# A two-block network on one core: the first modulation product as one phase of whole tiles instead of two halves

## What is computed

```python
c_act = jax.nn.silu(c)
mod = c_act @ w_ada[l] + b_ada[l]
sh1, sc1, gt1, sh2, sc2, gt2 = jnp.split(mod, 6, axis=-1)
u = _modulate(h, g_mix[l], sh1, sc1)
h = h + gt1[:, None, :] * _hybrid_mixer(u, w_in[l], ...)
u = _modulate(h, g_ffn[l], sh2, sc2)
h = h + gt2[:, None, :] * _conv_ffn(u, w_up[l], ...)
```

## Time and profile before

| what | value |
|---|---|
| median of 3 runs | 2468.82 us |
| the profiled execution | 2468.61 us, span 2466.8 us |
| PE busy, share of the span | 99% |
| PE weight loads | 81% |
| DVE, ACT, POOL busy | 47%, 37%, 43% |
| HBM read, whole kernel | 244.76 MB, 100 GB/s over the span |

### The profile page before, as it was taken

How to read it: one execution, slowest core, us unless ns; L and a number is a source line. 1 busy time by engine, 2 the same in 40 slices (tenths; PEclk the granted TensorE clock), 3 DMA queues, 4 the chain that set the end, 5 groups by cost and what they waited for, 6 DMA issues and landing times.

```text
span 2466.8 us, 32936 instructions
## 1 busy us (share of the span) xinstructions
PE 2453.8 (99%) x11477; PEld 2005.9 (81%) x11477; DVE 1168.4 (47%) x1728; ACT 914.3 (37%) x1307; POOL 1070.8 (43%) x529
## 2 busy tenths in 40 slices
PE   9999999999999999999999999999999999999999
PEld 6877888888888888877888888888888777888887
DVE  7574867256331345676330345331345666431332
ACT  4444443235322334555321334321234554431332
POOL 5332454444444445334444445444445334443444
PEclk9999999999999999999999999999999999999999
DMA  6223653332233331322232332233231332232332
GB/s 254 87 75 98 225 180 114 114 97 85 85 103 104 100 101 61 103 77 94 83 108 99 100 101 71 85 106 107 94 110 61 92 88 94 77 103 92 94 107 81
DMA packets 74062, 253.47 MB, mean 103 GB/s; under 512 B 9184, under 2 KB 13408, under 8 KB 73856
## 3 DMA queue, kind: packets, MB, share of 16 engines
q1 hardware_dynamic: 73408, 251.93, 31.6%
q10 hardware_dynamic: 576, 0.52, 0.1%
HBM read 244.76 MB, written 2.10 MB: 100 GB/s over the span
## 4 chain that ended last, share of the span: by engine, by line
PE 84%; issue 9%; DVE 3%; POOL 3%; ACT 1%; DMA 0%; SPq 0%; POOLq 0%; DVEq 0%; ACTq 0%
PE unit_bank L671 25%; PE unit_bank L673 25%; PE unit_bank L672 25%; POOL w_lo L530 2%; PE score L779 2%; PE score L769 1%; DVE arena L1772 1%; PE mix L672 1%; PE mix L673 1%; PE mix L671 1%; PE mix L927 1%; PE out_bank L906 1%; PE out_bank L726 0%; DVE arena L2521 0%; PE mix L1005 0%
## 5 line engine op out<-in xcount | busy, mean ns | idle before, releaser
L530 POOL TENSOR_TENSOR w_lo<-raw,w_hi 128x1024 fp32r<-128x1024 f32 (+2 forms) x374 | 953.8, 2550 | 1295.5 <-ACT w_hi L1268 1295.4
L1268 ACT ACTIVATE w_hi<-raw 128x1024 fp32r<-128x1024 f32 (+2 forms) x375 | 416.5, 1111 | 1163.9 <-PE unit_bank L673 1122.0
L671 PE MATMUL unit_bank<-u_hi,w_hi 128*128 128x512 f32 x2142 | 840.9, 393 | 0.4 <-POOL w_lo L530 0.4
L673 PE MATMUL unit_bank<-u_hi,w_lo 128*128 128x512 f32 x2142 | 835.2, 390 | 0.0
L672 PE MATMUL unit_bank<-u_lo,w_hi 128*128 128x512 f32 x2142 | 835.1, 390 | 0.0
L671 PEld LDWEIGHTS unit_bank<-u_hi,w_hi 128*128 128x128 f32 x2142 | 402.4, 188 | 93.6 <-issue 9.5
L673 PEld LDWEIGHTS unit_bank<-u_hi,w_lo 128*128 128x128 f32 x2142 | 402.4, 188 | 84.0
L672 PEld LDWEIGHTS unit_bank<-u_lo,w_hi 128*128 128x128 f32 x2142 | 402.6, 188 | 81.8 <-issue 0.2
L671 PE MATMUL unit_bank<-h_hi,w_hi 128*128 128x512 f32 x915 | 357.6, 391 | 0.2 <-DVE h_lo L2200 0.2
L673 PE MATMUL unit_bank<-h_hi,w_lo 128*128 128x512 f32 x915 | 356.6, 390 | 0.0
L672 PE MATMUL unit_bank<-h_lo,w_hi 128*128 128x512 f32 x915 | 356.6, 390 | 0.0
(11 more groups left out here) (422 smaller groups left out, 2176.7 us busy)
## 6 DMA issues: line engine op xcount, KB each, us to landing
raw<-in_w_gate_up SPq DMA_DIRECT2D x168, 512.0 KB, 3.5
raw<-in_w_down SPq DMA_DIRECT2D x64, 704.0 KB, 4.1
raw<-in_w_in SPq DMA_DIRECT2D x65, 512.0 KB, 3.5
raw<-in_w_up SPq DMA_DIRECT2D x30, 512.0 KB, 3.5
f<-in_w_ada_rows SPq DMA_DIRECT2D x26, 512.0 KB, 4.8
raw<-in_w_out SPq DMA_DIRECT2D x24, 512.0 KB, 3.6
raw<-in_w_down SPq DMA_DIRECT2D x16, 512.0 KB, 3.5
ada_in_u<-in_w_ada SPq DMA_DIRECT2D x8, 512.0 KB, 11.2
```

The lines of the kernel that those rows point to most:

```text
L530: e.tensor_tensor(w_lo[:, s, 0:n], raw[:, s, 0:n], as32(w_hi[:, s, 0:n]), ALU.subtract).then_inc(lo_ready, 1)
L671: e.matmul(bank[:], wh, hi(k), start=begin and n == 0, stop=False)
L673: mm = e.matmul(bank[:], wl, hi(k), start=False, stop=end and last)
L1268: e.activation(w_hi[:, s, 0:n], raw[:, s, 0:n], ACT.Copy).then_inc(hi_ready, 1)
```

## The change

w_ada is loaded in eight transfers of 1 MB, whole rows of 2048 columns in pieces of 8 KB, all of them issued ahead of the three tiles of w_in. Four land in the place of u_hi and u_lo, three in h, one in slots 16 to 19. `ada_part(k)` multiplies 512 columns into each quarter of the bank, once per k. The row has 512 columns, four transposes turn it, and DVE needs two short operations (`take_turned`, `amplify`) instead of two times three. `modulate` runs over all 8 chunks in one go. One part of `grow` stands ahead of it and one behind. POOL does all four doublings ahead of its splits. The group products are ordered anew: for each chunk the highs and rests of two units, the low of the first, and from the third chunk on the third unit two chunks behind; then the rest of the low parts.

```diff
-            load_ada_first(0, ada_loaded)
+            for k in range(DC):
+                e.dma_start(ada_first[k], d["w_ada"][k]).then_inc(ada_loaded[k], 16)
             for s in range(2):
                 load(0, s, d["w_in"][s], D)
             e.dma_start(third_raw[:], d["w_in"][2]).then_inc(third_loaded, 16)
-            load_ada_first(1, second_loaded)
...
-            for n in (1, 2):
+            for n in (1, 2, 4, 8):
                 double(n)
                 square_angle()
+            e.sem_inc(turn_ready, 1)
             split_pair(IN1, D)
             e.wait_ge(hi_ready, 3)
             e.tensor_tensor(third_lo[:], third_raw[:], as32(third_hi[:]), ALU.subtract).then_inc(lo_ready, 1)
-            e.wait_ge(B_padded, 1)
-            for n in (4, 8):
-                double(n)
-                square_angle()
-            e.sem_inc(turn_ready, 1)
...
-            def ada_part(half, k):
+            def ada_part(k):
...
                 for q in range(4):
-                    mm = e.matmul(out_bank[32 * q:32 * q + 32, 0:2 * P], c_act[:, k:k + 1].broadcast_to([P, 32]),
-                                  ada_first[half][k][:, 2 * P * q:2 * P * (q + 1)], start=k == 0, stop=k == DC - 1)
+                    mm = e.matmul(out_bank[32 * q:32 * q + 32, :], c_act[:, k:k + 1].broadcast_to([P, 32]),
+                                  ada_first[k][:, T * q:T * (q + 1)], start=k == 0, stop=k == DC - 1)
...
-                elif k == 5:
+                elif k == 4:
                     e.wait_ge(x0_inverse, 1)
...
-                else:
-                    keep_warm(2)
-            turn_ada(0, score[0], 2)
-            keep_warm(12, out_bank)
+                elif k < DC - 1:
+                    keep_warm(4)
+            turn_ada(0, score[0], TB)
+            keep_warm(10, out_bank)
...
+            e.wait_ge(uhi_ready, 1)
             for s in range(2):
                 e.wait_ge(hi_ready, s + 1)
                 e.wait_ge(taken[s], 1)
+                group_high(s, 0)
+            for c in range(1, DC):
+                both(group_high, c, uhi_ready)
+                both(group_rest, c - 1, u_ready)
+                e.wait_ge(lo_ready, 1)
+                group_low(0, c - 1)
+                if c >= 2:
+                    e.wait_ge(hi_ready, 3)
+                    group_high(2, c - 2)
+                    group_rest(2, c - 2)
+            both(group_rest, DC - 1, u_ready)
+            group_low(0, DC - 1, True)
+            e.wait_ge(lo_ready, 2)
+            for c in EIGHT:
+                group_low(1, c, c == DC - 1)
+            for c in (DC - 2, DC - 1):
                 group_high(2, c)
                 group_rest(2, c)
+            e.wait_ge(lo_ready, 3)
+            for c in EIGHT:
                 group_low(2, c, c == DC - 1)
...
-            take_row(DC, 0, out_bank[:, 0:2 * P])
+            take_row(DC, 0, out_bank[:])
             for s in range(2):
                 refill(IN1, s)
-            for s in range(2):
-                shifted(0, s)
+                shifted(s)
             e.wait_ge(third_loaded, 16)
             e.activation(third_hi[:], third_raw[:], ACT.Copy).then_inc(hi_ready, 1)
-            for c in range(2, 4):
-                shifted(0, c)
-            take_row(2 * DC, 1, out_bank[:, 0:2 * P])
-            for c in range(4, DC):
-                shifted(1, c)
+            for c in range(2, DC):
+                shifted(c)
...
-            take_half(0)
-            e.wait_ge(x0_spread, 1)
-            modulate(range(4))
             power_of_lam(2, 2)
             e.wait_ge(zeroed, 1)
-            grow(B_grown, STRIDE, b_bar[:, 0, :, :], b_bar[:, 1, :, :], False)
+            grow(B_grown, STRIDE, b_bar[:, 0, :, :], b_bar[:, 1, :, :], False, (0,))
+            take_turned(1, 0, score[0])
+            amplify(0, "g_mix", 8)
+            e.sem_inc(mod_ready, 1)
+            e.wait_ge(x0_spread, 1)
+            modulate(range(DC))
+            grow(B_grown, STRIDE, b_bar[:, 0, :, :], b_bar[:, 1, :, :], False, (1,))
             e.sem_inc(B_padded, 1)
-            take_half(1)
-            modulate(range(4, DC))
```

More of the change, by code:

```diff
@@ L208, in program @@
         ada_in_f = f.rearrange("p (n c) t -> p n (c t)", c=4)
-        ada_first = [[ada_in_u[:, k, :] for k in range(DC)],
-                     [ada_in_h[:, k, :] for k in range(6)] + [slot(16, 2), slot(18, 2)]]
+        ada_first = [ada_in_u[:, k, :] for k in range(4)] + [ada_in_h[:, k, :] for k in range(3)] + [slot(16, 4)]
         ada_gate = f.rearrange("p (n c) t -> p n (c t)", c=2)
         ada_shift = [ada_late[:], ada_in_f[:, 0, :], ada_in_f[:, 1, :]]
-        ada_row = [slot(20)[:, 0:2 * P], slot(20)[:, 2 * P:4 * P], slot(22)]
+        ada_row = [slot(20), slot(22)]
         gate_sum, shift_sum, gate2_sum = slot(20, 2), slot(18, 4), slot(24, 2)
@@ L251, in program @@
         ada_loaded = [sem(f"ada_loaded{i}") for i in range(DC)]
-        second_loaded = [sem(f"second_loaded{i}") for i in range(DC)]
         third_loaded = sem("third_loaded")
@@ L1008, in _ @@
             for k in EIGHT:
[L1009 removed]
+                ada_part(k)
                 if k == 3:
@@ L1018, in _, with both @@
                     mm.then_inc(x0_spread, 1)
-                else:
-                    keep_warm(2)
-            turn_ada(0, score[0], 2)
-            keep_warm(12, out_bank)
+                elif k < DC - 1:
+                    keep_warm(4)
+            turn_ada(0, score[0], TB)
+            keep_warm(10, out_bank)
+            def both(product, c, ready=None):
+                if ready is not None:
+                    e.wait_ge(ready, c + 1)
+                for s in range(2):
+                    product(s, c)
+            e.wait_ge(uhi_ready, 1)
             for s in range(2):
@@ L1401, in post_gain, with shifted @@
                 return lambda c: table[:, bass.ds(at + (2 * r - 1) * DC + c, 1)]
-            def shifted(half, c):
-                e.wait_ge(mod_ready, half + 1)
+            def shifted(c):
+                e.wait_ge(mod_ready, 1)
                 e.wait_ge(ux_ready, c + 1)
@@ L1804, in _ @@
             tt(fim, t1, rden, ALU.mult)
-            step(e.tensor_scalar(scale_bias, col("b_ada", 8, 8), 1.0, None, ALU.add))
             for c in range(0, DC, 2):
```

59 lines of the change are left out of this document (10 added, 49 removed).

## The result

The changed kernel takes 2473.26 us (median of 15 runs, 2472.02 to 2475.53), the kernel before 2468.78 us (15 runs, 2468.54 to 2470.03). The ratio is 1.002 with a 95% interval of 1.0013 to 1.0027: 4.5 us slower, just under the 0.2% that I wanted to call a difference, and as forecast. The profiled execution took 2472.45 us with a span of 2470.6, that is 3.8 us more span than before (2466.8), 0.7 less than forecast. The 15 runs are not one cloud: eight lie at 2472.0 to 2473.3 and seven at 2474.4 to 2475.5. The profiled one is of the first group. I come back to this, since it decides how much of the 4.5 us my sum really explains.

What follows compares the result with a forecast made beforehand. PE, busy 99%, was taken as the bound, so only the steady part's start shifts: last part 8.1 us later, 3.6 us gained behind it, net +4.5 us, giving 2473.3 us (0.18% slower), range 2471.5 to 2477.0.

Steps and rivals of the forecast that it cites:

- The basis: Whole kernel: later steps wait for PE or what it releases, so a start shift reaches the end unchanged.
- the marker: First weight load of the first whole unit: at 52.13 us before, forecast at 56.65 us.
- L: Landing of the last 1 MB w_ada part: 37.1 less 4.2 (w_in moved behind) and 1.4 (larger pieces), 31.5 us.
- The hold-up: Loads before the change: third_raw landed 1.5 us later than the rate gives; expected to persist largely with other data.
- The first rival: Start-up loads run quicker, without the 1.5 us delay or at 425 GB/s: 2471.8 to 2472.7 us; chance 0.2.
- L to U: Last part through ACT's copy, transposes and two DVE operations: 3.35 us.
- U: Start of the first DVE operation of `modulate`: 25.78 us before, forecast 34.85 us.
- U to the group's products: Early group products: chunk 2 starts at U + 5.1, then PE's pace, 14.8 us to U + 19.9.
- U to marker: From `modulate`'s start through group products and sixteen transposes to the first whole unit: 21.8 us.
- Costed at nothing: DVE's lambda power and half of `grow` (4.7 us), POOL's doublings (7 us), moved ahead of U: no cost.
- The clock rival: PE's clock falls in the DMA-bound start-up: +6.3 to +9.5 us, 2475.1 to 2478.3 us; chance 0.12.
- Faster: PE saves eight parts and DVE's break; pays only if L is below 27.9, near 500 GB/s; chance 0.03.

Runs made afterwards that it cites:

- first_tile_less: `warm_more` with only 128 columns of w_ada's first tile loaded and the second tile multiplied twice; 2469.97 us.
- small_pieces: The changed kernel with each w_ada tile loaded as two 512 KB transfers in pieces of 2 KB; 2474.56 us.
- warm_none: The changed kernel without the products that only keep PE busy between the parts and behind the turn; 2475.04 us.
- collision_forced: The changed kernel with `take_turned` done twice on DVE, so that `amplify` starts after POOL's first split; 2476.9 us.
- warm_more: The changed kernel with a few more products that only keep PE busy, placed in its waits; 2472.55 us.
- grow_inside: `warm_more` with the second part of `grow` put between chunks 3 and 4 of `modulate`; 2479.75 us.
- no_collision: The changed kernel with POOL's first split waiting until DVE's `amplify` is done; 2473.53 us.
- one_tile_less: The changed kernel with only 128 columns of w_ada's last tile loaded and the seventh tile multiplied again; 2472.52 us.
- weights_first: `warm_more` with the three w_in tiles loaded ahead of w_ada; 2476.62 us.

## Why the prediction was right, and where it was off

*The basis.* The shift of the start is the shift of the end: 3.6 at the marker, 3.8 in the span; and in `first_tile_less` one tile less in front is 2.4 to 2.6 us at the end. This held for the change. But not every later step waits for PE, as I had written: at 2011 us PE waits for a transfer, 0.47 us in this execution and up to 1.67 in others.

*L.* 31.4 against 31.5. In the traces the last bytes land 5.6 us earlier than before (5.6 booked). The pieces: sixteen landings 1.35 us apart became eight 2.49 us apart, 1.7 us less (booked 1.4; `small_pieces` gives 1.6). The three tiles of w_in: 3.8 us at the 1.28 us between their landings. The hold-up: before, third_raw lands 1.4 us late; now the seventh tile does, by 1.1, which leaves 0.3. These make 5.8, so 0.2 go elsewhere. With the 4.2 that I took for w_in I had kept 1.1 of the hold-up, and 1.1 came; that is partly luck, since it came at another transfer, and in the other six profiles with the same loads in the same order it measures 1.0 to 1.8 us in five and 0.3 in `warm_none`. The first rival (transfers quicker) gets 427 and 419 GB/s right and fails on this hold-up.

*L to U.* 3.1 to 3.2 (31.4 or 31.51 to 34.59) against 3.35; a little less in each hand-over.

*U to the group's products.* Chunk 2 at U + 4.64 instead of U + 5.1. This is the step that was mis-sized most, by 0.5 us: I had booked three more hand-overs of 0.1 and the longer durations of ACT. From there the pace is PE's as said: 16.5 us to the marker, against 14.8 + 1.9 = 16.7 in the sum. So U to marker is 21.2 instead of 21.8. With L to U this makes 0.8 us, and with 0.1 of L the 0.9 by which the marker is ahead of the forecast (55.76 against 56.65); 0.2 of it comes back behind the marker, which leaves the difference between the profiled execution (+3.8) and the forecast (+4.5).

*Costed at nothing.* The power of lambda and half of `grow` end at 30.4 us where I had 27.5, POOL's doublings at 31.3 where I had 29.7. Both are later than booked and still ahead of U, so they cost nothing, as said. What I had not asked is in which order the moved work and the unmoved work of POOL and DVE start. In the changed kernel the split of POOL and the `amplify` of DVE are released at the same time (34.26 both), and when `amplify` loses it waits for the end of the split: 0.17 us become 2.16 to 2.37. Shown: that this happens, what it costs (2.0 at the marker, `collision_forced`), that it happens in some executions and not in others (`first_tile_less` and `warm_more` with 2.36 and 0.17), and that PE idles behind it. In nanoseconds the traces put POOL's start first in all of these: by 2 to 5 ns in the seven profiles in which `amplify` keeps 0.17 us (the changed kernel: 5), by 6 and 7 ns in `grow_inside` and `first_tile_less`, in which it is held. Argued, and not shown: that it is what parts the 15 runs of the changed kernel. For it: the gap is 2.3 us between the middles of the groups; it is gone in `no_collision`; and it stays when the clock is equally low in every run (`warm_none`). Against: `warm_more` and `one_tile_less` change nothing in that race and yet have no and one run of the upper group in 11; with the collision excluded, runs at 2474.5 and 2475.88 are left, since the landing (1.3 us between profiles) and the wait at 2011 us (up to 1.2) can add up to as much; and six of the seven runs of the upper group have a mean clock of 0.999, so that part of their time may be the clock behind a waiting PE. No run of the upper group of the changed kernel was itself profiled.

So the median agrees with my number (+4.5) partly by luck: the mechanism I worked out gives +3.8 in the profiled execution, and the rest is the share of executions above it, which my sum had no term for.

The Trainium skill ("SBUF — State Buffer", section "SBUF: two separate sides") describes this: the port pair that DVE and GpSimd (POOL) share is an exclusive lock, taken for a whole instruction by whichever starts first, where DVE's operation has two SBUF inputs and GpSimd's reads SBUF; the other fully blocks. The traces agree on the block: 2.36 us beside a split of 2.35, while the operations of `modulate`, which read a PSUM bank, keep their 0.71 and 0.75 us beside the same splits. On who wins they agree from 6 ns on; at 2 to 5 ns `amplify` starts second by the record and is not held.

*The clock rival.* In the changed kernel the clock stays at 1.00 from 14 to 50 us in spite of the waits for the DMA (up to 1.5 us), with the busy-products between them; without these it falls (`warm_none`) and costs about 1 us. I had put 1.8 us on part and transposes alone; these did not come, since the clock was back at 1.00 for the last part (30.81 to U 33.89, 3.1 us as in the changed kernel) and a slow part ahead of it is hidden under the next landing. The Trainium skill ("TensorE: Matmul & The Clock Gate", section "Loop structure matters more than you think") speaks of a long wait for a DMA between every two products, after which PE is cold. My prediction left out the word "long" and so applied it too widely: the changed kernel's trace, with short waits and busy-products between them, does not contradict the page, and `weights_first`, with 5.9 us of wait ahead of the stretch at 0.58, agrees with it.

*Faster.* Nothing near it; the bytes would have had to come at 500 GB/s and came at 427 at most.

## What to carry to other kernels

Order loads by the byte that is needed last for the next engine to start: here all of w_ada stood ahead of the first products instead of half, and what was saved behind the landing (fewer parts, no break in DVE) was less than the 8 us that the start moved. Before shortening a transfer or a vector chain, look whether PE has a gap there at all; in the kernel before it had none, and landings 1.2 and 1.6 us earlier were worth nothing. When work is moved so that a DVE operation with two SBUF inputs and a GpSimd operation on SBUF become ready at the same moment, order them by a wait: the short one first cost nothing here from U to the marker, and otherwise some executions pay the whole of the long one (the median did not get better by it here). And read what an edit at the start does from a marker near it, not from one execution's whole time.

## What the runs showed that I had not expected

- A 128x8 operation of DVE took 2.16 to 2.37 us beside a GpSimd split of 2.35, against 0.17 when it started at most 5 ns behind the split. In the kernel before, the like operation took 0.16. It started 0.09 us ahead of the split, and it reads a PSUM bank (score) instead of mod, so by either it is not the same case:

```profile
25.46 0.16 DVE L1916 TENSOR_TENSOR amp<-score,cols 128x4 f32<-128x4 f32 x1
25.55 2.38 POOL L530 TENSOR_TENSOR w_lo<-raw,w_hi 128x1024 fp32r<-128x1024 f32 x1 [2.88 <-ACT w_hi L1268]
```

- One transfer of 1 MB lands 3.5 to 4.3 us after the one before it rather than 2.5, while the DMA engines are booked as busy. It is the seventh tile in the changed kernel and in seven others, also in `first_tile_less`, where it lands at 26.5 instead of 28.4 (`warm_more`). In `weights_first` no tile of w_ada is late (2.5 us between all eight), and in `warm_none` and `small_pieces` the delay is spread over several transfers. The last part starts anywhere from 30.8 to 32.1 us in kernels that ask for the same bytes in the same order. What holds it up wasn't tried and stays open.
- An idle PE in front of the bound stretch can cost twice. In `grow_inside` PE is busy for 0.13 us of the 2 us from 36 to 38, behind the first collision, and the granted clock then reads 0.59 (38 to 40 us), 0.84 (40 to 50) and 0.90 (50 to 60). But `collision_forced` (0.04 us of the 2 from 36 to 38) and `first_tile_less` (0.03 of the 2 from 34 to 36) keep 1.00 in every stretch behind it.
- PE's wait at about 2011 us, deep in code that is the same in all kernels, is 0.45 to 0.48 us in ten profiles and 1.43 to 1.67 in four. What makes it long stays open; in the kernels with the change SP spends 3.35 to 3.58 us on issuing the four transfers there in the long cases and 2.39 in the others.
